# A two-layer transformer block and a state-space block on one core: where the rotated queries of the second attention are split into high and low parts

## What is computed

```python
qa = apply_axial_rope(rmsnorm(qa, q_norm_g), cos_a, sin_a)      # first attention: 8 heads, 2 key heads
ka = apply_axial_rope(rmsnorm(ka, k_norm_g), cos_a, sin_a)
ya = blocked_attention(qa, ka, va, 1.0 / math.sqrt(GQA_HEAD_DIM))

qb = (rmsnorm(cq, q_a_norm_g) @ w_q_up).reshape(b, s, MLA_HEADS, MLA_QK_DIM)   # second attention
q_nope, q_rope = qb[..., :MLA_NOPE_DIM], qb[..., MLA_NOPE_DIM:]
q_rope = apply_axial_rope(q_rope, cos_b, sin_b)
kvb = (rmsnorm(ckv, kv_a_norm_g) @ w_kv_up).reshape(b, s, MLA_HEADS, MLA_NOPE_DIM + MLA_V_DIM)
k_nope, vb = kvb[..., :MLA_NOPE_DIM], kvb[..., MLA_NOPE_DIM:]
k_rope = apply_axial_rope(kr, cos_b, sin_b)                     # one rotated key part for all 8 heads
yb = blocked_attention(qb, kb, vb, 1.0 / math.sqrt(MLA_QK_DIM))
merged = g_a * (ya @ w_branch_a) + g_b * (yb @ w_branch_b)
```

## Time and profile before

| | |
|---|---|
| Time, median of 3 executions | 2894.73 us (2890.14 to 2894.97) |
| The profiled execution's own time | 2893.43 us |
| Its span in the trace | 2891.6 us |
| Mean granted TensorE clock | 0.988 of full speed |
| PE busy | 2804.2 us (97%) |
| DVE, ACT, POOL busy | 1597.0, 1173.1, 722.6 us |
| The two attention loops | about 50 to 262 us (layer 0) and 853 to 1062 us (layer 1) |

### The profile page before, as it was taken

One profiled execution on the slowest core, in us unless ns is written; L12 is line 12 of the kernel. 1 busy time (PEld: TensorE's weight loads), 2 busy tenths in 40 slices (PEclk: granted clock), 3 DMA queues, 4 the chain that ended last, 5 costly groups with the idle time before them and its releaser, 6 DMA issues.

```text
span 2891.6 us, 34995 instructions
## 1 busy us (share of the span) xinstructions
PE 2804.2 (97%) x13382; PEld 2322.0 (80%) x13382; DVE 1597.0 (55%) x2158; ACT 1173.1 (41%) x1869; POOL 722.6 (25%) x608
## 2 busy tenths in 40 slices
PE   8999999999999999999999999999999999999998
PEld 6677887888877778888888888888887779788887
DVE  5787446334267874464542885555434468555532
ACT  5676334222246663342222655332222348432222
POOL 2563013314015641133040240122100013122211
PEclk9999999999999999999999989999999989999999
DMA  4011322223221113223332212223232210132332
GB/s 140 30 44 44 119 96 83 97 95 97 100 81 37 37 44 122 96 81 102 100 97 95 73 57 76 96 95 98 99 106 92 87 44 1 59 102 95 98 103 99
DMA packets 75127, 239.90 MB, mean 83 GB/s; under 512 B 9264, under 2 KB 17728, under 8 KB 74976
## 3 DMA queue, kind: packets, MB, share of 16 engines
q1 hardware_dynamic: 73776, 234.46, 24.6%
q0 software_dynamic: 928, 3.27, 0.4%
q10 hardware_dynamic: 272, 0.06, 0.0%
HBM read 232.51 MB, written 2.10 MB: 81 GB/s over the span
## 4 chain that ended last, share of the span: by engine, by line
PE 86%; DVE 7%; ACT 3%; issue 2%; POOL 1%; DMA 1%; POOLq 0%; SPq 0%; DVEq 0%; ACTq 0%
PE bank L2171 27%; PE bank L2173 27%; PE bank L2172 27%; PE bank L2608 2%; PE bank L2423 1%; DVE X L1723 1%; DVE STAT L1827 1%; DVE UL L1711 1%; DVE FF L1718 1%; DMA RAWW<-weights 1%; DVE FF L1738 1%; PE bank L2512 1%; DVE WL L1694 0%; ACT WH L1330 0%; PE bank L2366 0%
## 5 line engine op out<-in xcount | busy, mean ns | idle before, releaser
L1694 DVE TENSOR_TENSOR WL<-RAWW,WH 128x1024 fp32r<-128x1024 f32 (+3 forms) x429 | 576.8, 1348 | 744.0 <-ACT WH L1330 743.6
L2171 PE MATMUL bank<-UH,WH 128*128 128x512 f32 (+2 forms) x1968 | 769.2, 391 | 27.3 <-DVE UL L1711 11.6
L2173 PE MATMUL bank<-UH,WL 128*128 128x512 f32 (+2 forms) x1968 | 760.5, 386 | 0.0
L2172 PE MATMUL bank<-UL,WH 128*128 128x512 f32 (+2 forms) x1968 | 759.8, 386 | 0.0
L1330 ACT ACTIVATE WH<-RAWW 128x1024 fp32r<-128x1024 f32 (+3 forms) x432 | 432.3, 1012 | 402.3 <-DMA RAWW<-weights 401.9
L2171 PEld LDWEIGHTS bank<-UH,WH 128*128 128x128 f32 (+1 forms) x1968 | 372.1, 189 | 111.2 <-issue 14.7
L2172 PEld LDWEIGHTS bank<-UL,WH 128*128 128x128 f32 (+1 forms) x1968 | 372.3, 189 | 76.2 <-issue 2.7
L2173 PEld LDWEIGHTS bank<-UH,WL 128*128 128x128 f32 (+1 forms) x1968 | 371.6, 189 | 75.2
L2171 PE MATMUL bank<-HH,WH 128*128 128x512 f32 (+1 forms) x576 | 210.8, 366 | 0.0
L2173 PE MATMUL bank<-HH,WL 128*128 128x512 f32 (+1 forms) x576 | 210.5, 365 | 0.0
L2172 PE MATMUL bank<-HL,WH 128*128 128x512 f32 (+1 forms) x576 | 210.5, 365 | 0.0
(11 more groups left out here) (365 smaller groups left out, 4689.9 us busy)
## 6 DMA issues: line engine op xcount, KB each, us to landing
RAWW<-weights SPq DMA_DIRECT2D x432, 512.0 KB, 3.5
X<-x SPq DMA_DIRECT2D x8, 256.0 KB, 4.9
FF<-tables POOLq DMA_DIRECT2D x2, 1024.0 KB, 7.2
U<-S5U SPq DMA_DIRECT2D x32, 64.0 KB, 2.0
out<-FF SPq DMA_DIRECT2D x16, 128.0 KB, 1.8
GEL<-U SPq DMA_DIRECT2D x64, 16.0 KB, 1.8
S5B<-s_b POOLq DMA_DIRECT2D x1, 512.0 KB, 4.5
S5C<-s_c POOLq DMA_DIRECT2D x1, 512.0 KB, 3.9
```

Source lines behind the costliest of these rows:

```text
L1694: dve.tensor_tensor(slot_words(WL, c % SLOTS, size), slot_words(RAWW, c % SLOTS, size), f32(slot_words(WH, c % SLOTS, size)), ALU.subtract ...
L2171: nc.tensor.matmul(out_, w[0], x_[0], start=start, stop=False, **how)
L2172: nc.tensor.matmul(out_, w[0], x_[1], start=False, stop=False, **how)
L2173: return nc.tensor.matmul(out_, w[1], x_[0], start=False, stop=stop, **how)
```

## The change

Three things are moved, and nothing is added or taken away.

1. `turn_out` of the second attention (ACT, MQH) stands behind the pass's exponential instead of ahead of it, and `turn_low` (DVE, MQL) behind the pass's maximum, reciprocal and `att_lo` instead of ahead of all three. Both stay in the same pass, and `turn_low` still stands ahead of `att_out_lo`.
2. The low part of the shared rotated key (`turn_low` of `kr`) goes from pass 23 to 24, and the two tables are scaled in passes 25 and 26 instead of 24 and 25 (POOL, L1117).
3. POOL clears the unused halves of the value tiles (`value_zeros`, four MEMSETs) in the pass of `mla_mm` of head 1 (30) instead of head 0 (26).

```diff
-        for m in range(HEADS):
-            if x == first[m] + 5:
-                plan.add("turn_out", **rotations[m])
-                plan.add("turn_low", **rotations[m])
         if x < n:
             plan.add("att_scores", "u", h=x // KT, t=x % KT)
         if 1 <= x <= n:
             plan.add("att_normalise", u=x - 1)
+        for m in range(HEADS):
+            if x == first[m] + 5:
+                plan.add("turn_out", **rotations[m])
         if 3 <= x <= n + 2:
             plan.add("att_transpose", u=x - 3, h=(x - 3) // KT, t=(x - 3) % KT)
@@
         if 4 <= x <= n + 3 and x != n:
             plan.add("att_lo", u=x - 4, h=(x - 4) // KT, t=(x - 4) % KT)
+        for m in range(HEADS):
+            if x == first[m] + 5:
+                plan.add("turn_low", **rotations[m])
         if 0 <= h < 2 * HEADS and phase == 3:
             plan.add("att_out_lo", h=h, pv=h)
@@
-    (22, "turn_out", "kr"), (22, "latent_low", "ckv0"), (23, "turn_low", "kr"), (23, "latent_low", "ckv1"),
-    (24, "scale_table", "cos"), (25, "scale_table", "sin")]
+    (22, "turn_out", "kr"), (22, "latent_low", "ckv0"), (23, "latent_low", "ckv1"), (24, "turn_low", "kr"),
+    (25, "scale_table", "cos"), (26, "scale_table", "sin")]
@@
-                elif st.kind == "mla_mm" and st.h == 0:
+                elif st.kind == "mla_mm" and st.h == 1:
                     value_zeros(l)
```

## The result

The changed kernel takes **2918.03 us** (median of 6, 2913.89 to 2920.40) against 2893.53 us before (median of 6, 2890.14 to 2894.97). The ratio is 1.0087, interval 1.0077 to 1.0097: 24.5 us slower, where 34 to 35 us were forecast. The time lies in the range of 2909 to 2939, between the likeliest case (2929) and the rival in which the clock holds (2914). The profiled execution took 2917.22 us (span 2915.4, mean clock 0.987); all its lines stand two further down than before's.

What follows compares the result with a forecast made beforehand. PE was taken as the bound, 86% of the chain of waits. Terms 24.5 - 1.3 - 4.0 + 15.2 = 34.4 us on the profiled 2893.4 gave 2927.8, with the median 1.3 higher 2929 us; range 2909 to 2939.

Steps and rivals of the forecast that it cites:

- the likeliest case: Four to eleven clock drops behind the 14 new PE stalls; 2929 us, own range 2920 to 2936, chance 0.6.
- the rival in which the clock holds: The new PE stalls come, with three clock drops or fewer; 19.2 us slower, 2914 us; chance 0.2.
- The chain over PE, DVE, ACT, DVE closes in one pass: Heads 1 to 7: exponential, MQH, MQL, PE's scores chain within a pass; scores start 2.15 us after E, the exponential's start.
- Heads 1 to 7, +24.5: Change 1 on seven heads per layer: first values come 1.73 or 1.87 us later per head, 24.5 us lost in all.
- the eighth, -1.3: Change 1 on each layer's last head: low part and bank copy no longer late, 0.7 us gained per layer.
- partly hidden: Rival: PE makes up most of each new stall in the rest of the head; about 2895 us, chance 0.04.
- faster: Rival: MQL still comes before PE needs it, if E comes at least 2.3 us earlier; 2889 us, chance 0.04.
- MQL doesn't meet POOL's multiply: Heads 1 to 7: POOL's multiply ends 0.25 us before MQL starts, so MQL stays at 0.69 us.
- Changes 2 and 3, -2.4 for the wait and -1.6 for the clock: Around pass 25: PE's low-part wait costs 1.2 us less per layer, layer 0's clock drop goes; -4.0 us together.
- The clock, +15.2: Eight of the 14 new PE stalls bring the clock down to 1.2 GHz, 1.9 us each; +15.2 us, bounds 0 and 39.

Runs made afterwards that it cites:

- experiment 1: The changed kernel with only the heads' reordering (change 1) kept, changes 2 and 3 undone; 2922.33 us.
- experiment 8: The kernel before with changes 2 and 3 and the new order of turn_out and turn_low for each layer's last head only; 2888.70 us.
- experiment 4: The changed kernel with turn_out (MQH) back ahead of the exponential on ACT, turn_low (MQL) left behind on DVE; 2907.14 us.
- experiment 2: The kernel before with only changes 2 and 3, the rotated queries left as before; 2891.12 us.
- experiment 3: The kernel before with only change 3, POOL's clearing of the value tiles in pass 30 instead of 26; 2893.61 us.
- experiment 6: The changed kernel with all side work of the second attention's heads one pass earlier, order inside a pass unchanged; 2897.88 us.
- experiment 10: The changed kernel executed once more, unaltered, for a second profile; 2917.59 us.
- experiment 5: The changed kernel with turn_low moved once more, behind att_out_lo of the same pass; 2917.51 us.

## Why the prediction was right, and which term was off

- *The chain over PE, DVE, ACT, DVE closes in one pass.* Right: scores at E + 2.14 for 2.15 and all 14 stalls came, of 2.72 us on the first head of a layer and of 2.28 us on the six after it, for 2.7 and 2.3 forecast in turn. From head 2 to head 7 the first scores come every 14.0 us (178.59 to 248.65 in five steps); before it was 12.3 (173.44 to 234.88). That is 1.7 us lost for each head, for the 1.8 forecast.
- *Heads 1 to 7, +24.5, and the eighth, -1.3.* Right, a little high: 21.8 us for their sum of 23.2 (experiment 1), and -1.2 for the eighth alone (experiment 8). That puts the new stalls of heads 1 to 7 near the lower bound of 23 us. Nothing of the stalls is made up later, which kills the rival "partly hidden"; "faster" fails by its own condition, E does not come earlier: it follows PE's first scores matmul of the pass by 1.62 us in both kernels (157.85 and 159.47; before, 159.75 and 161.37).
- *MQL doesn't meet POOL's multiply.* Right by 0.24 us in the changed kernel (MQL 0.69 us). It was a narrow escape: 0.8 us earlier it takes 1.16 (experiment 4). The Trainium skill, "GPSIMD Engine Reference", section 8 (Key points), has operations with two SBUF inputs contend with GpSimd; experiment 4 agrees, with 0.47 us on 0.69 where about 0.6 us of the multiply lay beside it.
- *Changes 2 and 3, -2.4 for the wait and -1.6 for the clock.* About right. The wait was worth 1.7 us over the two layers (experiment 2), and 1.9 by the difference of changed and heads only, of whose 3.51 us a stretch at 1.2 GHz takes 1.6; the bounds of 0.5 to 1.9 per layer hold, and the 1.2 taken was above the 0.9 measured. The drop behind the stall at 139.67 had cost 1.5 us. In its new place PE's wait of 1.02 us is left, since the second MKL and the maximum behind it hold the low part of pass 25. The 2.54 us of POOL's idle time are a row of pass 31, not of the passes to which the tables and the clearing moved; the clearing cost nothing there all the same (experiment 3).
- ***The clock, +15.2: wrong in size.*** This is the step that failed. Three of the 14 new stalls brought the clock down and not eight, and they cost 3.0 + 1.6 + 1.6 = 6.2 us, where 15.2 was taken. The price of one drop was right (2.1 on average, for 1.9); the number was not. Less what the clock had taken in the kernel before, the net is +4.0 us where 15.2 - 1.6 = 13.6 was taken; with 20.1 us of waits (20.8 forecast) that makes the 24.1 us that the loops grew by.

Three new drops are also what the forecast had left to a rival: its likeliest case was four to eleven drops (0.6), "the clock holds" was three or fewer (0.2). So the case that came is that rival, at 2918 where it said 2914; 2918 lies in the range because the range was made wide enough to hold both, and not because the likeliest case was right.

Why the share was wrong shows when the stalls of all twelve traces (before, changed and the ten experiments) in the attention loops are sorted by length, from start to start less the time of the matmuls between (those over 1.75 us), and those counted at whose end, or within 4 us of it, the clock fell:

| stall | how many | clock fell |
|---|---|---|
| 1.89 to 2.04 us | 18 | 1 |
| 2.25 to 2.33 us | 50 | 8 |
| 2.41 to 2.61 us | 22 | 14 |
| 2.68 to 2.72 us | 8 | 5 |

The six stalls of the earlier trace rows were lumped into one share, four of six. Twelve of the 14 new ones are 2.28 us long, and for that length the share is one in six, not four in six. Behind longer ones it is higher, but that length is the cause is not shown: the rows of 2.41 us and more are nearly all the first and the last heads, which have other work around them, and several traces share the same program or most of it. The one drop behind a stall of 2.04 us, that of the kernel before, was an exception, and experiment 3 shows the same stall without it. One drop more is in no row of the table, the one of experiment 6 behind two stalls under 0.9 us. With these shares the term would have been 12 x 0.16 + 2 x 0.6 = 3.1 drops of 1.6 us, 5.0 us, and the forecast about 2919 us; the counts contain this result, so they explain it and don't foretell it. In the Trainium skill, "TensorE: Matmul & The Clock Gate", section "Why this matters for your kernels", gaps above about 3 us are what is said to bring the clock down; these rows contradict that, with drops behind stalls of 2.3 us, once of 2.04 us, and in experiment 6 behind two of 0.9 us. By the rule the time would have been 2914 us, 4 us short; by my share it was 11 us too long. What decides between two stalls of one length stays open: it repeated in one repeated execution of the program (experiment 10) and did not in one that differs in the order of two operations on DVE alone (experiment 5). That it is a matter of when a stall falls was only argued; no run here sets that time on purpose.

## What to carry to other kernels

A step that feeds the next pass of a pipeline must not stand behind anything that waits for the current pass: PE then stands for the chain's whole length less what it has to do in between. Here the chain is 2.15 us, PE stood for 2.28 us, and 1.7 us of that was lost for good on each head. Idle time ahead of an instruction on DVE or ACT is not slack if what ends it comes from PE. The old place was the best one for seven heads of eight, so an order is worth choosing per head: only the last, whose input is late anyway, gained from the new one.

## What the runs showed that I had not expected

- The clock falls behind some stalls of 2.3 to 2.7 us and not behind others (the table above), and once behind two of 0.9 us; a stretch of 3.4 us at 1.2 GHz mostly costs 1.4 to 1.6 us.
- DVE's two-input subtraction of 96x512 took 1.16 us instead of 0.69 beside POOL's 1.04 us multiply, seven heads out of eight in experiment 4.
- Two orders on DVE that differ by a 0.69 us operation gave the same start of PE (161.61 and 161.64), since the displaced one fits into the 0.77 us wait for ACT.
